# Attention by row tiles from the last to the first, two heads at a time, with routing beside it and the first norm's root as a power on GpSimd

## The reference

```
proj  = h @ w_in                                # 1024 -> 256 pool, 3 x 384 q k v, 768 conv
A     = causal pooling with windows 2, 4, 8, 16
B     = attention of 6 heads x 64, three dilated windows with ALiBi, merged by their denominators
C     = GLU -> causal depthwise conv with 31 taps -> LN -> swish
x     = LN1(2 ** 0.25 * h + concat(A, B, C) @ w_o)
logits = x @ router_w + router_b; top 4 of 32 experts, softmax over the 4
x     = LN2(2 ** 0.25 * x + sum of gate * expert(x))       # SwiGLU expert, 1024 -> 2048, 1024 -> 1024
```

## Time and profile before

| what | value |
|---|---|
| device time, three runs | 1388.15, 1389.2, 1391.41 us (median 1389.2) |
| span of the profiled execution, first to last instruction | 1387.7 us |
| PE busy | 1208.0 us (87%) |
| DVE, ACT, POOL busy | 511.4, 268.4, 295.4 us |
| the DMA engines, mean over the span | 334 GB/s |
| L1754 and L1768, the experts' matmuls | 590.1 + 299.0 us |
| L836, the projections | 100.9 us |

### The profile page before, as it was taken

How to read it: one execution, slowest core, us unless ns; L and a number is a source line. 1 busy time by engine, 2 the same in 40 slices (tenths; PEclk the granted TensorE clock), 3 DMA queues, 4 the chain that set the end, 5 groups by cost and what they waited for, 6 DMA issues and landing times.

```text
span 1387.7 us, 33845 instructions
## 1 busy us (share of the span) xinstructions
PE 1208.0 (87%) x12380; PEld 531.4 (38%) x12381; DVE 511.4 (37%) x860; ACT 268.4 (19%) x520; POOL 295.4 (21%) x263
## 2 busy tenths in 40 slices
PE   6998989883799999999989898998998989997860
PEld 5886434461223333343333333342342323432230
DVE  1996624275432222224222322232223230422226
ACT  0013223220011111131111131031121111131112
POOL 7000112624120222004112131114121212120113
PEclk9999999975999999999999999999999999998975
DMA  9600840282999999999999999999999999999963
GB/s 338 198 3 31 279 178 3 85 319 73 412 416 418 412 409 403 419 415 399 416 417 410 415 408 416 383 417 401 415 411 412 410 419 410 388 405 420 410 229 124
DMA packets 78667, 463.12 MB, mean 334 GB/s; under 512 B 11876, under 2 KB 19657, under 8 KB 28333
## 3 DMA queue, kind: packets, MB, share of 16 engines
q1 hardware_dynamic: 67915, 438.55, 77.7%
q0 software_dynamic: 8656, 17.87, 5.1%
q10 hardware_dynamic: 2066, 6.32, 1.2%
HBM read 448.29 MB, written 19.48 MB: 337 GB/s over the span
## 4 chain that ended last, share of the span: by engine, by line
PE 52%; DMA 18%; issue 3%; DVE 2%; SPq 0%; ACT 0%; DVEq 0%; ACTq 0%; POOLq 0%
PE pu L1754 32%; PE rest L1768 17%; DMA ring<-in_e_in 11%; DMA ring<-in_e_out 7%; PE pu L1748 1%; PE rest L1779 1%; DVE fin L1970 0%; DVE bn L1952 0%; DVE xgT L1891 0%; DVE mv L1963 0%; DMA acc_rows<-y,row 0%; SPq L270 0%; ACT y L1834 0%; PE rest L1773 0%; DMA fin<-acc_rows 0%
## 5 line engine op out<-in xcount | busy, mean ns | idle before, releaser
L1754 PE MATMUL pu<-ring,xgT 128*32 128x512 f32 x5248 | 590.1, 603 | 34.0 <-DMA ring<-in_e_in 33.2
L1754 PEld LDWEIGHTS pu<-ring,xgT 128*32 128x32 f32 x5248 | 161.9, 111 | 445.0 <-issue 444.3
L1768 PE MATMUL rest<-ring,hid 128*32 128x256 f32 x5248 | 299.0, 386 | 15.5 <-DMA ring<-in_e_out 11.0
L1677 POOL DMA_INDIRECT acc_rows<-y,row x82 | 110.5, 1347 | 778.7 <-ACT y L1834 762.6
L1921 DVE TENSOR_SCALAR gg<-pu 128x1280 f32<-128x1280 f32 x32 | 47.7, 1492 | 603.8 <-PE pu L1754 603.8
L1768 PEld LDWEIGHTS rest<-ring,hid 128*32 128x32 f32 x5248 | 170.8, 111 | 134.1 <-issue 31.0
L1834 ACT ACTIVATE y<-rest,gate 32x256 f32 x328 | 152.8, 466 | 286.1 <-issue 282.4
L1814 ACT ACTIVATE ss<-gg 128x1280 f32<-128x1280 f32 x32 | 40.7, 1271 | 545.1 <-DVE gg L1921 545.1
L836 PE MATMUL pair<-xt,ring 128*128 128x260 f32 x448 | 100.9, 388 | 12.6 <-DMA ring<-in_w_in 12.6
L1667 POOL DMA_INDIRECT xq<-x_rows,idx x82 | 87.1, 1062 | 58.0 <-issue 46.1
L836 PEld LDWEIGHTS pair<-xt,ring 128*128 128x128 f32 x448 | 86.5, 194 | 25.8 <-DMA ring<-in_w_in 12.3
(11 more groups left out here) (266 smaller groups left out, 619.7 us busy)
## 6 DMA issues: line engine op xcount, KB each, us to landing
ring<-in_e_in SPq DMA_DIRECT2D x256, 1024.0 KB, 23.1
ring<-in_e_out SPq DMA_DIRECT2D x128, 1024.0 KB, 24.6
ring<-in_w_in SPq DMA_DIRECT2D x3, 1536.0 KB, 24.1
ring<-in_w_in SPq DMA_DIRECT2D x6, 512.0 KB, 12.6
xt<-in_xT SPq DMA_DIRECT2D x2, 1040.0 KB, 11.2
ring<-in_w_o SPq DMA_DIRECT2D x1, 2048.0 KB, 12.0
conv<-in_x_prompt SPq DMA_DIRECT2D x1, 2048.0 KB, 14.7
x_rows<-conv ACTq DMA_DIRECT2D x4, 512.0 KB
```

Of the source, the lines that this page charges most:

```text
L1677: nc.gpsimd.indirect_dma_start(out=acc_dram, out_offset=bass.IndirectOffsetOnAxis(ap=row4[0:GS, u % AHEAD, j:j + 1], axis=0), in_=y[at, u ...
L1754: mm = nc.tensor.matmul(pu[quarter(c), j], xgT[:, j, k], w[:, :, c * QC:(c + 1) * QC], start=False, stop=k == KT - 1, skip_group_check=True)
L1768: mm = nc.tensor.matmul(py[quarter(c), j], hid[:, j, 2 * q + f], w[:, f, c * QC:(c + 1) * QC], start=False, stop=q == FT // 2 - 1 and f == ...
```

## The change

1. Order of the attention. 12 steps instead of 24: tile 3 for the three pairs of heads, then tiles 2, 1, 0. A step computes both heads of a pair; the scores of the two use partitions 0 to 63 and 64 to 127 of the contraction, one after the other, and the values are alternating matmuls on columns 0 to 63 and 64 to 127 of the array, 128 rows wide each.
2. The output projection's rest, the norm, the transposes, the logits and the ranks of tiles 3, 2 and 1 stand between the steps of the attention of later tiles (`REST_AT`, `TURN_AT`, `LOGITS_AT`, `RANK_AT`); only tile 0 follows at the end.
3. The multiplication by the row sum's reciprocal goes from POOL to DVE; the bias and the queries change sign, so that the maximum becomes a minimum and the instruction that negated it goes.
4. The root of the first norm's variance: instead of Sqrt on ACT and a reciprocal on DVE, `pow` with the exponent -0.5 on POOL.
5. `wo4` and the sample rows' `v` use groups of 32 columns of the array side by side: 32 matmuls of 256 columns for 16 of 512, and 24 of 128 for 8 of 384.
6. The first transfers are split into halves of the contraction, and PE starts on the first. POOL's bias DMAs wait for the last part of `xt`. The down bias is fetched with the up bias, into `mix`, and split right after it, early in the program; DVE waits for it (`drow_ready`) before it writes the conv's output there.
7. Three more of the first expert's ring units are loaded earlier (units 4, 5, 6).

```diff
+TILES = (3, 2, 1, 0)
+NPAIR = NH // 2
+NSTEPS = NPAIR * NT
+SCORED_AT, PROBS_AT, VALUES_AT, SUMS_AT, WO4_AT, TURN4_AT, LOGITS4_AT, RANK4_AT = 0, 2, 3, 4, 5, 6, 7, 8
+PART_AT = {6: 0, 7: 1, 4: 2, 5: 4, 2: 6, 3: 7, 0: 9, 1: 10}
+REST_AT = {3: 5, 2: 8, 1: 11}
+TURN_AT = {3: 6, 2: 9, 1: 12}
+LOGITS_AT = {3: 7, 2: 10, 1: 13}
+RANK_AT = {3: 9, 2: 12}
...
-            sp.dma_start(xt[:, :, 0:HALF], xT[:, :, 0:HALF]).then_inc(ld["xt"], 16)
-            proj_cols("gate0", c0 + CONVW, c0 + CONVW + P)
+            for name, ks in (("first", slice(0, KT // 2)), ("second", slice(KT // 2, KT))):
+                sp.dma_start(xt[:, ks, 0:HALF], xT[:, ks, 0:HALF]).then_inc(ld[f"xt_{name}"], 16)
+                sp.dma_start(wtile[:, gate0, ks], w_in[:, (c0 + CONVW) // P:(c0 + CONVW) // P + 1, ks]
+                             ).then_inc(ld[f"gate0_{name}"], 16)
...
+            gp.wait_ge(ld["xt2"], 16)
             for part in range(3):
                 gp.dma_start(btok[part * NE:(part + 1) * NE], o["e_brow"]).then_inc(ld["brow"], 16)
-            gp.wait_ge(zeroed, 4)
+            for part in range(3):
+                gp.dma_start(otok[part * NE:(part + 1) * NE], o["e_bout"][0]).then_inc(ld["bout"], 16)
...
-            for n in range(nsteps):
-                gp.wait_ge(s_recip, n + 1)
-                w = (n % NT + 1) * P
-                nc.gpsimd.tensor_scalar(pr[:, n % 3, 0:w], pr[:, n % 3, 0:w], negm[:, 3, n:n + 1], None, ALU.mult
-                                        ).then_inc(normed, 1)
...
+                nc.gpsimd.tensor_tensor(mv[0:m, 2:3], mv[0:m, 1:2], minus_half[0:m, :], ALU.pow).then_inc(rstd_ready, 1)
...
             def scores(n):
+                i, hp = TILES[n // NPAIR], n % NPAIR
+                w = (i + 1) * P
+                for h in range(2):
+                    lo = HD * h
+                    if n >= 1:
+                        pe.wait_ge(s_max, 2 * n - 1 + h)
+                    nc.tensor.matmul(bS[h][:, 0:w], qT[lo:lo + HD, hp, i * P:(i + 1) * P], kT[lo:lo + HD, hp, 0:w],
+                                     start=True, stop=True).then_inc(qk_done, 1)
...
             def values(n):
...
                 for j in range(i + 1):
+                    for h in range(2):
+                        mm = nc.tensor.matmul(pv[HD * h:HD * h + HD, 0:P],
+                                              v[:, j, (2 * hp + h) * HD:(2 * hp + h + 1) * HD],
+                                              pt[:, n % 2, h, j * P:(j + 1) * P], start=j == 0, stop=j == i,
+                                              skip_group_check=True)
...
+            def row_norms(n):
+                w = (TILES[n // NPAIR] + 1) * P
+                for h in range(2):
+                    at = 2 * n + h
+                    d.wait_ge(exp_done, at + 1)
+                    ch.do(V.reciprocal(negm[:, 3, at:at + 1], negm[:, 2, at:at + 1]))
+                    V.tensor_scalar(sc[:, n % 2, h, 0:w], sc[:, n % 2, h, 0:w], negm[:, 3, at:at + 1], None, ALU.mult
+                                    ).then_inc(normed, 1)
```

More of the change, by code:

```diff
@@ L722, in _ @@
                 evac_kt(i)
-            evac_v(NT)
+            stepped(a, f"v{NT}")
+            for c in range(ATTW // P):
+                ins = nc.scalar.activation(v[0:NS, NT, c * P:(c + 1) * P], bank(f"v{NT}")[c * GS:c * GS + NS, 0, 0:P], ACT.Copy)
+            ins.then_inc(freed(f"v{NT}"), 1)
             def sample_softmax():
@@ L1039, in values @@
-            def values(h):
-                b = begin(f"pv{h // 2}") if h % 2 == 0 else bank(f"pv{h // 2}")
-                lo = HD * (h % 2)
-                pe.wait_ge(pt_done, NT * (h + 1))
-                for j in range(NT):
-                    mm = nc.tensor.matmul(b[lo:lo + HD, 0, j * P:SEQ], v[:, j, h * HD:(h + 1) * HD],
-                                          pt[:, h % 2, j, j * P:SEQ], start=j == 0, stop=j == NT - 1)
-                mm.then_inc(pe_step if h % 2 else pv_even, 1)
@@ new lines, in rank @@
+            def rank(i):
+                pe.wait_ge(m_ready, NTH[i])
+                pe.wait_ge(small_read, SMALL.index(f"r{i}"))
+                at = ranks_of(i)
+                nc.tensor.matmul(at, trib[0:NS, 1], memb[0:NS, NT], start=True, stop=False)
+                for j in TILES[:NTH[i] - 1]:
+                    mm = nc.tensor.matmul(at, trib[:, 0 if j == i else 1], memb[:, j], start=False, stop=j == i)
+                mm.then_inc(rank_done, 1)
+            for n in range(NSTEPS + 2):
+                if n < NSTEPS:
@@ L1125, in _ @@
+                if n >= 2:
+                    values(n - 2)
+            out_rest(0)
+            rank(1)
+            turn_rows1(0)
+            logits(0)
+            rank(0)
+            pe.wait_ge(s_max, 2 * NSTEPS)
             for j in range(NT + 1):
[L1126 removed]
+                mm = nc.tensor.matmul(totals, trib[0:rows(j), 1, 0:NE], memb[0:rows(j), j],
                                       start=j == 0, stop=j == NT)
```

559 lines of the change are left out of this document (285 added, 274 removed).

## The result

| | before | changed |
|---|---|---|
| median of 4 runs each, same chip | 1390.2 us | 1376.3 us |
| profiled execution's span | 1387.7 | 1373.5 |
| first matmul of PE | 12.63 | 5.33 |
| DVE's first product | 29.19 | 22.27 |
| PE takes up the means (last conv result) | 109.98 | 119.46 |

The change is faster: ratio 0.9894, 95% interval 0.9872 to 0.9916, or 13.9 us. That is small, but clear of the noise. The forecast was 8.6 us (1380.6, range 1369 to 1391): its direction and its frame held; every part of the sum before the experts was mis-sized, and the errors cancelled in part. Two executions further down, one of e1 at 1483.6 us and one of e7 at 1591.0, ran in a slow state of the chip and are left out of all times and ratios.

What follows compares the result with a forecast made beforehand. The experts' weight streaming was taken as a fixed 1050.2 us block, starting 8.6 us earlier: start and taps +8.3, sample v -0.8, loop and end -16.1. That gave 1380.6 us, range 1369 to 1391.

Steps and rivals of the forecast that it cites:

- frame: Experts' stretch: the last 1050.2 us move as a whole, so only the first expert matmul's start counts.
- Part A: Program start: DVE's first product comes at 24.3 us against 29.2, gain 4.9 us, bounds 3 and 6.
- by about 13.3: Program start: time in us when both halves of xt and gate0 are loaded, with the bias put off.
- Part B: Conv taps on DVE: POOL's bias splits beside them cost 16.4 us, 13.2 more than now.
- the sharing by fixed parts of the time: Conv taps: a POOL subtraction takes 0.50 of DVE's time beside it, a cast 0.22.
- rival 4: Conv taps: DVE and POOL block each other for whole instructions; loss 23.1 us, time 1387.3, chance 0.05.
- Rival 2: Conv taps: POOL costs them nothing like this; attention starts 13 us earlier, time 1367.4, chance 0.15.
- about 0.094 us: Sample rows' v before the attention: time per instruction for 48, 4.5 us in place of 5.33, -0.8.
- Part C: Attention loop: PE's work is 101.2 us; tile 1's rest ends 106.2 us after the attention's start, at 275.4.
- rival 3: Attention loop: scores of two heads don't run together; +8.8 us, time 1389.4, chance 0.07.
- Rival 1: PE in the loop: short values don't overlap their weight loads; 18 us more, time 1399, chance 0.14.
- Part D: Tail from tile 1's rest to the first expert matmul: a chain of 53.5 us, ending at 328.9.

Runs made afterwards that it cites:

- e1: Changed kernel with the down bias loaded later and split by POOL in the attention's first steps, off the taps; 1370.3 us, ratio 0.9860 to before.
- e7: Changed kernel with the attention's end reordered: last transposes, values and tile 0's rest run during tile 1's norm; 1364.9 us, ratio 0.9824 to before.
- e12: Changed kernel with the splits of both biases in POOL instructions of 256 columns; 1381.1 us, ratio 0.9942 to before.
- e3: Changed kernel without POOL's wait for the second half of xt before it asks for the bias rows; 1374.5 us, ratio 0.9890 to before.
- e10: Changed kernel with xt's first half and gate0's weights loaded in one transfer each, the bias still waiting; 1381.1 us, ratio 0.9936 to before.
- e2b: Changed kernel with the splits of both biases moved into the attention and ring unit 4 loaded later; 1360.4 us, ratio 0.9778 to before.
- e11: Changed kernel with the up bias split in POOL instructions of 2048 columns instead of four of 512; 1381.7 us, ratio 0.9944 to before.
- e4: Changed kernel with the norms' root back on ACT as a square root, plus a reciprocal on DVE; 1373.4 us, ratio 0.9875 to before.
- e9: Changed kernel with a small matmul between the two heads' scores of each step, so they can't run together; 1390.5 us, ratio 1.0012 to before.
- e13: Changed kernel with only the up bias split in POOL instructions of 256 columns, the down bias's staying at 1024; 1373.4 us, ratio 0.9884 to before.
- e8: Changed kernel with both bias splits moved into the attention and the attention's end reordered; 1346.3 us, ratio 0.9682 to before.

## Why the prediction was right, and where it was off

**The frame held.** The experts' stretch was a block in all kernels but e12. The gain lies where the sum put it, behind the attention's start, and the start and the taps together cost time: attention +3.5 us (forecast +7.5), from there to the first expert -18.2 (forecast -16.1), stretch +0.4. Together that is -14.2 us of span.

**Part A** was undersized: 6.9 us for 4.9, and beyond its own bound of 6. The first product came at 22.27. The mis-sized term is the arrival of the input, "by about 13.3": POOL asks for the bias, which waits for the last part of xt, at 11.65. With the 3.65 and 7.3 us that the sum has for PE this gives 22.6. e3 shows that it is the bias' delay that makes the gain, e10 that the halves add 2.7 to it.

**Part B**: the loss was 19.5 us, for 16.4. The step that failed is the sharing by fixed parts of the time, a half beside a subtraction and 0.22 beside a cast. The two engines take turns by instructions, which was rival 4, given 0.05. That the forecast of the loss came near was luck in this: most of POOL's subtractions have the 512 columns of the row that the share was read from, and at that length turns and halves agree. e1 divides the loss. The up bias cost 12.4 us, where the forecast's shares give 11.2, and the down bias 7.1, where they give 5.2: by turns a subtraction of 1024 columns costs 1.7 us, not 1.2, and a cast 0.6, not 0.4. Rival 2 falls with e1, e2b and e11. Rival 4's size, 23.1, was too high, as shown above. Hidden behind the taps, PE's 12.62 us of waiting cost nothing, as said; without the loss (e2b) it is gone.

**From the last conv result to the attention** the prediction moved everything unchanged except v. It took 45.8 us, where it had been 51.8 and 51.0 were forecast. The sample rows' v takes 1.93 us: "about 0.094 us" an instruction was 0.04, which is 3.4 gained for 0.8. The other 2.6 come from the variance at the full clock (2.87 for 5.54), which was luck, since no edit aimed at it, and e3 and e4 have it at 4.53 and 4.56. An idle gap of 0.6 us ahead of the first scores is gone as well, and the way from the means to the variance is 0.8 longer:

```profile
133.98 2.87 PE L899 MATMUL pair<-conv,cst 128*128 128x260 f32 x12 [2.27 <-ACT conv L736]
```

**Part C**: 99.5 us for 106.2. The scores came as forecast, a pair of tile 3 in 1.13 us, and rival 3 falls with this row and with e9. The values took 0.065 us an instruction for 0.10, 108 x 0.035 = 3.8 less; wo4 took 3.6 us for 6.0. PE's idle time is 4.7 of the 5 allowed. These make up the difference but for 0.2. Rival 1 is out: the values' weight loads take 0.145 us each on average, and 16 values come in 1.09, so the loads overlap each other and the matmuls. No run takes back the new order of the tiles alone, or DVE's multiplication; for these there is only the sum of PE's rows. PE's timeline in the loop (to the earlier trace rows):

```profile
165.27 1.13 PE L1066 MATMUL bS<-qkv 64*128 64x512 f32 x4
184.25 1.09 PE L1090 MATMUL pair<-ring,qkv 128*64 128x128 f32 x16
201.75 3.64 PE L1027 MATMUL pair<-ring,mix 128*8 128x256 f32 x64
205.32 5.42 PE L1016 MATMUL pair<-ring,mix 128*128 128x512 f32 x12
```

**Part D**: 58.0 us for 53.5. The power was taken at 0 and cost 0.54 us in each of two tiles. The other 3.4 are the low clock, for which the prediction had allowed 1 us up to the end of tile 0's rest. The tail's rows (to the earlier trace rows):

```profile
267.58 1.53 POOL L681 TENSOR_TENSOR mv<-mv,minus_half 128x1 f32<-128x1 f32 x1 [8.13 <-DVE mv L1339]
269.23 1.28 DVE L1348 SCALAR_TENSOR_TENSOR conv<-conv,mv,xt 128x1024 f32<-128x1024 f32 x1 [0.54 <-POOL mv L681]
270.57 1.97 PE L1101 MATMUL bT<-cst,conv 128*128 128x128 f32 x8 [4.77 <-DVE conv L1348]
274.88 3.62 PE L1044 MATMUL pair<-rw,xt 128*128 128x32 f32 x16
279.06 7.31 PE L1016 MATMUL pair<-ring,mix 128*128 128x512 f32 x12
...
322.82 1.05 PE L1808 MATMUL pu<-brow,chosen 128*32 128x512 bf16 x8 [11.31 <-DVE xgT L1951]
```

The logits of tile 1 take 3.62 us, where tile 2's took 1.97 in the loop, and tile 0's rest 7.31 for 5.42, both behind a wait of 4.77. The errors of part A, of the way to the attention and of part C (2.0 + 5.2 + 6.7) outweigh those of B and D (3.1 + 4.5). That leaves some 6 us more gain than the sum had, and a forecast nearer than its terms were.

## What to carry to other kernels

Where DVE bounds, look at what POOL does beside it: POOL's instructions are paid by nearly their whole lengths, so move them to a stretch that another engine bounds (16 us here) rather than tune them. If they must stay, short pieces cost the taps less than long ones (loss 14.7 us in e13, 19.5, and 25.0 in e11). But added instructions can cost elsewhere (e12), and e13's gain didn't show in its time. A transfer that is put off also puts off the work that waits for it: ask what that work will then lie beside. Where an engine waits for one norm after another, look for work that is queued behind the wait but doesn't need it: here this made the tail 13 us shorter, and some of the work ran at the full clock as well.

## What the hardware showed that was not expected

Short matmuls on groups of columns follow each other every 0.04 us (the sample rows' v, 48 of 128 columns in 1.93 us) and 0.057 (wo4, 64 of 256 in 3.64), each with a weight load of its own. A power of 128x1 on POOL takes 1.54 us if POOL has been waiting for it, and 0.58 if it comes to it after other work (tile 2's, at 245.07 in the changed kernel); ACT's root takes 0.20. The low clock (granted clock 0.5) mostly comes after a wait of PE, but not after each: parts in the loop of 4.56 us were 6.3 to 6.6 in e1, e2b and e10 and not in the changed kernel or e8, with the same order around them. And it can come without a wait. In e9 the granted clock is 0.50 from 202 to 205 us, though PE's timeline shows no wait in the 18 us before, and a part takes

```profile
201.27 6.23 PE L1007 MATMUL pair<-ring,mix 128*128 128x512 f32 x10
```

in place of 4.54. Such stretches moved single kernels by 2 to 5 us, which is as much as some of the edits. What sets them off was not tried.
